# Suffix sums of stick-breaking attention: full fp32 products or split-operand products

## The chip, the cores and the metric

One core of a Trainium2 chip runs the whole kernel. The metric is device time in microseconds from launch to end; several runs are taken and the median is compared. The profile names the engines: PE (TensorE, matrix products) with its weight loads PEld, DVE (VectorE), ACT (ScalarE), POOL (GpSimd), SP (SyncE). Each engine works through its own list of instructions in order, and semaphores tie the lists together.

## What is computed

One layer of a streaming encoder for 512 new prompt frames and 32 frames of a running stream (with 512 cached keys and values). The input projection feeds gMLP gating and stick-breaking attention (8 heads of 64); an output projection and a mixture of 16 experts follow. The part that matters here:

```
def stick_breaking(q, k, v, q_pos, k_pos):
    z = jnp.einsum('bqhd,bshd->bhqs', q, k).astype(jnp.float32) * (SB_HEAD_DIM ** -0.5)
    causal = k_pos[None, :] < q_pos[:, None]
    log_beta = jax.nn.log_sigmoid(z)
    log_keep = jnp.where(causal, log_beta - z, 0.0)
    rest = lax.cumsum(log_keep, axis=3, reverse=True) - log_keep
    w = jnp.where(causal, jnp.exp(log_beta + rest), 0.0)
    return jnp.einsum('bhqs,bshd->bqhd', w.astype(v.dtype), v)
```

With s = softplus(z), the exponent of a weight is z minus the sum of s over this key and all later ones up to the query. So a reversed running sum over keys is needed for each query.

## The kernel before, in words

The kernel lies in one function, with one list of instructions per engine. Attention stands between the input projection (five column blocks, ends near 174 us in the profile) and the output projection (begins near 249 us).

Scores are kept transposed: keys on the 128 partitions, queries along the columns. There are nine passes, called heads here: pass 0 is the sample group with all its heads side by side, passes 1 to 8 are the eight prompt heads. For a prompt head the four key chunks of 128 need 512, 384, 256 and 128 query columns (causal), 1280 in all, in three PSUM banks: chunk 0 fills the first bank (512), chunks 1 and 3 the second (384 + 128), chunk 2 the third (256). Two sets of banks take turns, so the scores of head h+2 must wait until the weights of head h have been read out of the same banks.

For each head the steps are:

- scores (PE, L1475 and the mask product L1477): full fp32 products of the keys with the queries. A full fp32 product shows as two records of PE.
- absolute value (DVE, `abs_z`, L1000), then exp(-|z|) (ACT, L708) and log(1 + .) (ACT, L713) in `lw`; the 512-column bank first, then the other 768 columns.
- softplus (DVE, `softplus`, L1014): max(z, 0) plus that logarithm, from PSUM and SBUF into the tile `sp`; then three additions (L1030) that sum later key chunks for chunks that need more than one of them, into `later`.
- suffix sums (PE, `suffix_sums`): products of `negU` (-1 on and below the diagonal) with a chunk's own softplus (L1503, 1280 columns) and of `negones` (all -1) with the softplus of later chunks, summed by DVE where it can (L1513, 768 columns). They accumulate onto the scores in PSUM, all as full fp32 products.
- weights (ACT, `weights`, L782): exp of the banks into `lw`.
- values (PE, `values`, L1532, for pass 0 L1543): products of weights and values, for two heads at a time, half of them before each of the next heads' scores. ACT and DVE then write the result as a high and a low part (`sb_hi` L787, `sb_lo` L1089) for the output projection.

The order of PE in the loop over heads is written out by hand: part of the values of earlier heads (from head 4 on), scores of head h+1, suffix sums of head h; behind the loop the remaining values. DVE's order is absolute value and softplus of head h+1, and at heads 5 and 7 the low part of an attention output, at head 7 also a weight split. ACT's is exponentials and logarithms of head h+1, then weights of head h. POOL does nothing between 155 and 249 us. The weight loads of the experts on SP's queue start when the last values are done.

Projections already use split operands: an operand x is written as a high part of type fp32r (ACT, `whi`) and a low part x - high (DVE or POOL, `wlo`), and three products high x high, high x low, low x high replace one full fp32 product. Their products are L1384 to L1386; POOL's subtractions of low parts are L555 (512 columns), L564 (2048) and, in the expert stage, L591 (1024).

Of the kernel before, what the change touches and what calls it, by code (L numbers as in the profile page):

```python
# [34 lines left out]
def trunk_step(nc, x_prompt, x_sample, cache_k, cache_v, norm1_g, w_in, gm_v_norm_g, gm_w_s, gm_b_s,  # L35
# [34 lines left out]
    with ExitStack() as ctx:  # L70
# [19 lines left out]
        negU = sb("negU", [P, P])  # L90
        negones = sb("negones", [P, P])
# [37 lines left out]
        gvn = sb("gvn", [P, NT, CB], stack=mix)  # L129
# [13 lines left out]
        ZW = 1280  # L143
# [3 lines left out]
        sp = [sb(f"sp{i}", [P, ZW], stack=st_b) for i in range(2)]  # L147
        later = sb("later", [P, 6 * P], stack=st_b)
# [70 lines left out]
        later_ok = sem("later_ok")  # L219
# [60 lines left out]
        s_regions = [(c * DW // 512, c * DW % 512, DW, c) for c in range(NCH + 1)]  # L280
# [9 lines left out]
        def later_sums(h):  # L290
            return later[:, 3 * P * (h % 2):3 * P * (h % 2 + 1)] if h else later[:, :]
# [168 lines left out]
        def _(pool):  # L460
# [35 lines left out]
            link(pool.memset(negU[:, :], -1.0))  # L496
            pool.memset(negones[:, :], -1.0)
            pool.affine_select(out=negU[:, :], in_=negU[:, :], compare_op=ALU.is_ge, fill=0.0, base=0,
                               pattern=[[-1, P]], channel_multiplier=1).then_inc(pc, 1)
# [28 lines left out]
            for b in range(2):  # L528
# [3 lines left out]
                for t in range(NT):  # L532
# [6 lines left out]
                    pool.tensor_tensor(q3, q3, g, ALU.mult).then_inc(qk_ok, 1)  # L539

# [108 lines left out]
        def _(act):  # L649
# [52 lines left out]
            def exp_log(h):  # L702
                b_ = lw[h % 5]
                pieces = [[b_[:, 0:512]], [b_[:, 512:ZW]] if h else [b_[:, 512:1024], b_[0:DEC, 1024:ZW]]]
# [236 lines left out]
        def _(dve):  # L941
# [62 lines left out]
            def softplus(h):  # L1004
# [3 lines left out]
                s, u = sp[h % 2], later_sums(h)  # L1008
                if h == 0:
                    link(dve.memset(s[:, 1024:ZW], 0.0))  # L1010
# [6 lines left out]
                dve.wait_ge(sp_ok, h + 1)  # L1017


                n = P if h else DW  # L1020
                if h == 1:
                    dve.wait_ge(rest_ok, 2)
                if h:
                    adds = ((2, s[:, 1152:1280], s[:, 896:1024]), (1, s[:, 768:896], u[:, 2 * P:3 * P]),
                            (0, s[:, 640:768], s[:, 1024:1152]))
                else:
                    adds = ((2, s[:, 768:1024], s[:, 1024:1280]), (1, s[:, 512:768], u[:, 2 * n:3 * n]),
                            (0, s[:, 256:512], u[:, n:2 * n]))
                for k, a, b in adds:
                    ins = dve.tensor_tensor(u[:, k * n:(k + 1) * n], a, b, ALU.add)  # L1030
                    if k:
                        link(ins)
                ins.then_inc(later_ok, 1)
# [321 lines left out]
        def _(pe):  # L1355
# [102 lines left out]
            def scores(h):  # L1458
# [12 lines left out]
                if h:  # L1471
                    for bk, c0, n, c, q0 in regions:
                        if h >= 2 and c == 1:
# [5 lines left out]
                        if bk == 0:  # L1479
                            mm.then_inc(z_ok, 1)  # L1480
                else:
                    pe.wait_ge(ckT_ok, NCH)
                    for bk, c0, n, c in s_regions:
# [5 lines left out]
                        if c == 1:  # L1489
                            mm.then_inc(z_ok, 1)  # L1490
                    mm = pe.matmul(z[bk][0:DEC, c0:c0 + n], identb[0:DEC, 0:DEC], maskneg8[:, :, :].rearrange("p h n -> p (h n)"),
                                   start=False, stop=True, skip_group_check=True)
                mm.then_inc(z_ok, 1)

            def suffix_sums(h):

                z, s = z_of(h), sp[h % 2]
                pe.wait_ge(sp_ok, h + 1)
                pe.wait_ge(pc, PC_U)
                u = later_sums(h)  # L1500
                for bk, c0, n, c, *_ in (regions if h else s_regions):
                    p = P if h or c < NCH else DEC
                    pe.matmul(z[bk][0:p, c0:c0 + n], negU[0:p, 0:p], s[0:p, 512 * bk + c0:512 * bk + c0 + n],  # L1503
                              start=False, stop=True, skip_group_check=True)
                pe.wait_ge(later_ok, h + 1)
                if h:
                    rest = ((0, P, s[:, 512:512 + P]), (0, 2 * P, u[:, 0:2 * P]), (1, P, s[:, 1024:1024 + P]),
                            (1, 2 * P, u[:, 2 * P:3 * P]), (2, P, s[:, 896:1024]))
                else:
                    rest = ((0, 0, u[:, 0:DW]), (0, DW, u[:, DW:2 * DW]), (1, 0, u[:, 2 * DW:3 * DW]),  # L1510
# [241 lines left out]
```

## Time and profile before

| | us |
|---|---|
| median of 3 runs | 530.46 |
| lowest and highest run | 530.32, 533.29 |
| span of the profiled execution | 529.8 |
| PE, DVE, ACT, POOL busy in it | 448.5, 291.5, 241.3, 194.1 |
| mean granted clock of PE | 0.940 |

The page gives the profiled execution by its span, from the first to the last instruction; no separate time of that execution is shown, and the median of the runs is 0.66 us above the span. In a timeline row the first number is the start from the span's beginning, the second the time that the row covers, "xN" the number of instructions merged into it, and the bracket the idle time of that engine before it with what ended it. Consecutive matrix products overlap in their records, so their pace is read from start to start. "out<-in" are the program's tile names without buffer numbers; the tile `lw` appears as `ckT` and `cv` where these are reused for it.

### The profile page before, as it was taken

How to read it: one execution, taken by the hardware profiler on the slowest of the kernel's cores; microseconds unless marked ns; L12 is line 12 of the kernel's file. 1: busy time of each engine (PE TensorE's matmuls, PEld its weight loads, DVE VectorE, ACT ScalarE, POOL GpSimd, SP SyncE). 2: the span in 40 equal slices, each digit the busy share in tenths (PEclk: the TensorE clock that was granted, in tenths of full speed). 3: DMA queues.
4: the chain of work that ended last, by engine and by line, in shares of the span. 5: the costliest groups of instructions: out<-in, count | busy, mean ns of one | idle time of the engine just before them, and what ended most of it. 6: DMA issues, size and time to landing. Idle time of an engine off the chain costs nothing. (4 is left out here: it accounts for less than half of the span.)

```text
span 529.8 us, 7155 instructions
## 1 busy us (share of the span) xinstructions
PE 448.5 (85%) x2569; PEld 333.4 (63%) x2569; DVE 291.5 (55%) x411; ACT 241.3 (46%) x330; POOL 194.1 (37%) x189
## 2 busy tenths in 40 slices
PE   1899999998979899999999961689999999999300
PEld 1677887777758576656777861466766766666200
DVE  2626332443243446565150747269898898998136
ACT  4625121343333536456113531167787777876100
POOL 3442100474540000001000761266767767746261
PEclk9999999998979999999999986599999999999855
DMA  8547202222331300000297397359999999993267
GB/s 300 165 72 280 62 24 81 83 77 80 119 125 56 109 1 1 1 1 1 90 390 275 128 354 242 91 191 338 342 348 330 331 344 316 362 366 131 85 228 277
DMA packets 61700, 95.31 MB, mean 180 GB/s; under 512 B 9265, under 2 KB 42033, under 8 KB 61665
## 3 DMA queue, kind: packets, MB, share of 16 engines
q1 hardware_dynamic: 47040, 69.48, 38.7%
q0 software_dynamic: 5088, 17.89, 10.4%
q10 hardware_dynamic: 9536, 7.50, 4.3%
q8 instruction: 19, 0.31, 0.2%
q14 instruction: 17, 0.13, 0.1%
HBM read 81.82 MB, written 13.04 MB: 179 GB/s over the span
## 5 line engine op out<-in xcount | busy, mean ns | idle before, releaser
L1272 DVE TENSOR_TENSOR wlo<-raw,whi 128x2048 fp32r<-128x2048 f32 (+1 forms) x45 | 96.9, 2154 | 24.4 <-ACT whi L866 24.4
L1384 PE MATMUL bank<-whi,xT_hi 128*128 128x512 f32 x224 | 93.6, 418 | 2.5 <-issue 1.9
L1385 PE MATMUL bank<-wlo,xT_hi 128*128 128x512 f32 x224 | 90.8, 405 | 0.0
L1386 PE MATMUL bank<-whi,xT_lo 128*128 128x512 f32 x224 | 90.8, 405 | 0.0
L866 ACT ACTIVATE whi<-raw 128x2048 fp32r<-128x2048 f32 x45 | 86.0, 1912 | 6.2 <-PE bank L1386 6.2
L591 POOL TENSOR_TENSOR wlo<-raw,whi 128x1024 fp32r<-128x1024 f32 x16 | 59.6, 3724 | 34.4 <-ACT whi L866 34.4
L953 DVE TENSOR_TENSOR wlo<-raw,whi 128x2048 fp32r<-128x2048 f32 x14 | 32.0, 2287 | 52.6 <-ACT whi L657 52.6
L1384 PE MATMUL bank<-whi,xsT_hi 128*96 128x512 f32 x128 | 53.4, 417 | 4.4 <-DVE xsT_lo L1278 3.1
L1384 PEld LDWEIGHTS bank<-whi,xT_hi 128*128 128x128 f32 x224 | 43.6, 195 | 14.6 <-issue 4.2
L1386 PE MATMUL bank<-whi,xsT_lo 128*96 128x512 f32 x128 | 51.4, 402 | 0.0
L1385 PE MATMUL bank<-wlo,xsT_hi 128*96 128x512 f32 x128 | 51.3, 401 | 0.0
L1386 PEld LDWEIGHTS bank<-whi,xT_lo 128*128 128x128 f32 x224 | 43.7, 195 | 10.5
L1385 PEld LDWEIGHTS bank<-wlo,xT_hi 128*128 128x128 f32 x224 | 43.7, 195 | 9.2
L657 ACT ACTIVATE whi<-raw 128x2048 fp32r<-128x2048 f32 x14 | 26.7, 1908 | 45.5 <-PE bank L1406 43.1
L545 POOL MEMSET wr_pad<- 128x1024 f32 x1 | 1.0, 956 | 95.4 <-issue 95.4
L478 POOL TENSOR_SCALAR ssq<-ssq 128x1 f32<-128x1 f32 (+3 forms) x25 | 5.0, 201 | 79.7 <-DVE ssq L1063 47.7
L1384 PEld LDWEIGHTS bank<-whi,xsT_hi 128*96 128x96 f32 x128 | 21.0, 164 | 18.2 <-issue 7.1
L578 POOL COPY idx_cur<-idx_all 96x1 int32<-96x1 int32 (+1 forms) x16 | 20.1, 1255 | 21.3 <-PE bank L1644 11.4
L1384 PE MATMUL bank<-whi,aT_hi 128*96 128x512 f32 x64 | 26.1, 408 | 1.8 <-DVE aT_lo L1288 1.1
L1386 PEld LDWEIGHTS bank<-whi,xsT_lo 128*96 128x96 f32 x128 | 21.1, 165 | 9.3
L1385 PEld LDWEIGHTS bank<-wlo,xsT_hi 128*96 128x96 f32 x128 | 21.2, 166 | 7.1
L480 POOL TENSOR_TENSOR rstd<-ssq,mhalf 128x1 f32<-128x1 f32 (+3 forms) x25 | 24.7, 988 | 2.1
(214 smaller groups left out, 773.2 us busy)
## 6 DMA issues: line engine op xcount, KB each, us to landing
raw<-in_w_gate_dram SPq DMA_DIRECT2D x32, 512.0 KB, 6.3
raw<-in_w_up_dram SPq DMA_DIRECT2D x32, 512.0 KB, 7.8
raw<-in_w_down_dram SPq DMA_DIRECT2D x32, 512.0 KB, 7.2
raw<-in_w_in_dram SPq DMA_DIRECT2D x10, 1024.0 KB, 5.4
expert_rows<-yout POOLq DMA_DIRECT2D x16, 384.0 KB
raw<-in_w_out_dram SPq DMA_DIRECT2D x4, 1024.0 KB, 5.1
x_sb<-in_x_prompt_dram SPq DMA_DIRECT2D x4, 512.0 KB, 8.8
normed_tokens<-xn ACTq DMA_DIRECT2D x4, 512.0 KB, 2.7
```

What stands on the lines that cost most here:

```text
L478: link(pool.tensor_scalar(s, s, 1.0 / width, EPS, ALU.mult, ALU.add))
L480: return pool.tensor_tensor(dst, s, mhalf[0:s.shape[0], 0:n], ALU.pow)
L545: link(pool.memset(wr_pad[:, :, :], 0.0))
L578: pool.tensor_copy(idx_cur[p][:, :], idx_all[:, bass.ds(i, 1)]).then_inc(idx_cp, 1)
L591: pool.tensor_tensor(wlo[split][:, D:2 * D], eraw[slot][:, D:2 * D], whi[split][:, D:2 * D].bitcast(F32), ALU.subtract).then_inc(m_lo_pool, 1)
L657: act.activation(whi[n % 2][:, :], raw[n % 3][:, :], ACT.Copy).then_inc(hi_ok, 1)
L866: act.activation(whi[SPLIT_OF[m3]][:, :], eraw[slot][:, :], ACT.Copy).then_inc(m_hi, 1)
L953: dve.tensor_tensor(wlo[n % 2][:, :], raw[n % 3][:, :], whi[n % 2][:, :].bitcast(F32), ALU.subtract)\
L1272: dve.tensor_tensor(wlo[SPLIT_OF[m3]][:, 0:n], eraw[slot][:, 0:n], whi[SPLIT_OF[m3]][:, 0:n].bitcast(F32), ALU.subtract).then_inc(m_lo, 1)
L1384: pe.matmul(acc, x_hi, w_hi, start=start, stop=False)
L1385: pe.matmul(acc, x_hi, w_lo, start=False, stop=False)
L1386: return pe.matmul(acc, x_lo, w_hi, start=False, stop=stop)
```

## The change

The suffix sums become split-operand products; scores, values and everything else stay as they are.

- Softplus is written in place over the logarithm (`lw`). DVE copies it, rounded, to `s_hi` (fp32r). The low part `s_lo` is softplus minus `s_hi`: of the first bank ("head", 512 columns) by DVE, of the other two ("tail", 768 columns) by POOL. `negU` and `negones` become fp32r, their values being exact in it.
- The three additions on DVE are gone. Instead PE multiplies `negones` with the softplus of each later chunk separately, once with the high and once with the low part: 20 products per head instead of 9.
- The order is turned: tail first, head second, in scores, absolute values, exponentials, logarithms, softplus, sums and weights. Products are ordered so that those with the same stationary tile stand together.
- PE now waits for the high parts, for POOL's low part of the tail and for DVE's low part of the head. ACT's wait before the weights goes. The narrow own chunk of the sample group (32 keys) keeps a full fp32 product with a small triangle `negU_s`.
- `s_hi` and `s_lo` of odd heads lie where `gvn` was, so DVE waits before head 1's softplus for the transposes of `gvn` (`gm_tr`).

```
...
-        regions = [(0, 0, 512, 0, 0), (1, 0, 384, 1, 128), (1, 384, 128, 3, 384), (2, 0, 256, 2, 256)]
+        regions = [(1, 0, 384, 1, 128), (1, 384, 128, 3, 384), (2, 0, 256, 2, 256), (0, 0, 512, 0, 0)]
...
-            return [(0, P, slice(0, 512))] if a == 0 else [(1, P, slice(512, 1024)), (2, p, slice(1024, ZW))]
+            return [(0, P, slice(0, 512))] if a else [(1, P, slice(512, 1024)), (2, p, slice(1024, ZW))]
+        def stored_parts(h, a):
+            if a:
+                return [(P, slice(0, 512))]
+            return [(P, slice(512, ZW))] if h else [(P, slice(512, 1024)), (DEC, slice(1024, ZW))]
...
+            for h in range(NH):
+                pool.wait_ge(s_hi_ok, 2 * h + 1)
+                for p, c in stored_parts(h, 0):
+                    ins = pool.tensor_tensor(s_lo[h % 2][0:p, c], lw[h % 5][0:p, c], s_hi[h % 2][0:p, c].bitcast(F32), ALU.subtract)
+                ins.then_inc(s_lo_tail, 1)
...
             def weights(h):
-                act.wait_ge(sp_ok, h + 1)
...
                 if h >= 2:
                     dve.wait_ge(rest_ok, 2 * (h - 1))
+                elif h == 1:
+                    dve.wait_ge(gm_tr, NT)
+                b_, hi, lo = lw[h % 5], s_hi[h % 2], s_lo[h % 2]
                 for a in range(2):
                     dve.wait_ge(l_ok, 2 * h + a + 1)
                     for bk, p, c in parts_of(h, a):
-                        ins = dve.scalar_tensor_tensor(out=s[0:p, c], in0=z_of(h)[bk][0:p, 0:c.stop - c.start], scalar=0.0,
-                                                       in1=lw[h % 5][0:p, c], op0=ALU.max, op1=ALU.add)
-                ins.then_inc(sp_ok, 1)
...
-                for k, a, b in adds:
-                    ins = dve.tensor_tensor(u[:, k * n:(k + 1) * n], a, b, ALU.add)
...
+                        ins = dve.scalar_tensor_tensor(out=b_[0:p, c], in0=z_of(h)[bk][0:p, 0:c.stop - c.start], scalar=0.0,
+                                                       in1=b_[0:p, c], op0=ALU.max, op1=ALU.add)
+                    ins.then_inc(sp_ok, 1)
+                    dve.wait_ge(sp_ok, 2 * h + a + 1)
+                    for p, c in stored_parts(h, a):
+                        ins = dve.tensor_copy(hi[0:p, c], b_[0:p, c])
+                    ins.then_inc(s_hi_ok, 1)
+                dve.wait_ge(s_hi_ok, 2 * h + 2)
+                dve.tensor_tensor(lo[:, 0:512], b_[:, 0:512], hi[:, 0:512].bitcast(F32), ALU.subtract).then_inc(s_lo_head, 1)
...
             def suffix_sums(h):
+                def own(chunks, s):
+                    for c in chunks:
+                        bk, c0, n, q0 = place[c]
+                        mm = pe.matmul(z[bk][:, c0:c0 + n], negU[:, :], s[:, 512 * bk + c0:512 * bk + c0 + n],
+                                       start=False, stop=True, skip_group_check=True)
+                    return mm
+                def later(chunks, s):
+                    for c in chunks:
+                        bk, c0, n, q0 = place[c]
+                        for c2 in range(c + 1, len(place)):
+                            b2, d0, n2, q2 = place[c2]
+                            p = DEC if c2 == NCH else P
+                            at = c0 + q2 - q0
+                            mm = pe.matmul(z[bk][:, at:at + n2], negones[0:p, :], s[0:p, 512 * b2 + d0:512 * b2 + d0 + n2],
+                                           start=False, stop=True, skip_group_check=True)
+                    return mm
+                hi, lo = s_hi[h % 2], s_lo[h % 2]
+                tail, head = ((3, 2, 1), (0,)) if h else ((3, 2), (1, 0))
+                pe.wait_ge(s_hi_ok, 2 * h + 1)
+                own(tail, hi)
...
+                later(tail, hi)
+                pe.wait_ge(s_lo_tail, h + 1)
+                later(tail, lo)
+                own(tail, lo).then_inc(rest_ok, 1)
+                pe.wait_ge(s_hi_ok, 2 * h + 2)
+                own(head, hi)
+                later(head, hi)
+                pe.wait_ge(s_lo_head, h + 1)
+                later(head, lo)
+                own(head, lo).then_inc(rest_ok, 1)
...
```

## Rows read from the trace of the kernel before

**Rows 1.** Table of stretches: busy us (instructions) per engine, PEclk, DMA share, GB/s.

```profile
220.00:240.00 20.00, 20.00 (x102) 12.77 (x100) 11.15 (x23) 10.83 (x19) 0.00 (x0) 1.00 0.00 1
```

**Rows 2.** Timeline of one head: start, duration, engine, line; in brackets idle before.

```profile
219.33 1.12 PE L1475 MATMUL bank<-qpad,kT 128*128 128x512 f32 x2
...
220.62 0.69 DVE L1000 TENSOR_SCALAR lw<-bank 128x512 int32<-128x512 int32 x1 [0.76 <-PE bank L1477]
...
221.34 0.63 ACT L708 ACTIVATE lw<-lw 128x512 f32<-128x512 f32 x1 [2.26 <-DVE lw L1000]
...
221.98 2.38 PE L1503 MATMUL bank<-sp,negU 128*128 128x512 f32 x8
222.18 1.02 DVE L1000 TENSOR_SCALAR lw<-bank 128x512 int32<-128x512 int32 x2 [0.87 <-PE bank L1477]
...
223.24 0.84 ACT L708 ACTIVATE lw<-lw 128x768 f32<-128x768 f32 x1 [1.26 <-DVE lw L1000]
...
223.99 1.34 ACT L713 ACTIVATE lw<-lw 128x512 f32<-128x512 f32 x2
224.19 0.38 PE L1513 MATMUL bank<-sp,negones 128*128 128x128 f32 x2
...
224.70 1.69 DVE L1014 SCALAR_TENSOR_TENSOR sp<-bank,lw 128x512 f32<-128x512 f32 x3 [1.50 <-ACT lw L713]
...
225.61 0.64 PE L1532 MATMUL bank<-ckT,v_sb 128*64 128x512 f32 x1
...
226.84 0.70 PE L1475 MATMUL bank<-qpad,kT 128*128 128x512 f32 x1
```

**Rows 3.** Timeline of DVE: the absolute values of heads 3 and 8.

```profile
199.00 0.69 DVE L1000 TENSOR_SCALAR ckT<-bank 128x512 int32<-128x512 int32 x1 [0.18 <-PE bank L1477]
...
235.63 0.69 DVE L1000 TENSOR_SCALAR ckT<-bank 128x512 int32<-128x512 int32 x1 [0.76 <-PE bank L1477]
```

**Rows 4.** Timeline of PE: split-operand products of 512 columns, back to back.

```profile
172.06 0.40 PE L1384 MATMUL bank<-whi,xT_hi 128*128 128x512 f32 x1
172.30 0.40 PE L1385 MATMUL bank<-wlo,xT_hi 128*128 128x512 f32 x1
```

**Rows 5.** Groups of DVE by form, 160 to 260 us: the additions between SBUF tiles.

```profile
L1030 DVE TENSOR_TENSOR later<-sp 128x128 f32<-128x128 f32 x16 | 4.7, 292 | 0.5
...
L1030 DVE TENSOR_TENSOR later<-sp,later 128x256 f32<-128x256 f32 x2 | 0.8, 424 | 0.1
```

**Rows 6.** Groups of POOL by form: its low-part subtractions (busy us, mean ns).

```profile
L591 POOL TENSOR_TENSOR wlo<-raw,whi 128x1024 fp32r<-128x1024 f32 x16 | 59.6, 3724 | 34.4 <-ACT whi L866 34.4
...
L564 POOL TENSOR_TENSOR wlo<-raw,whi 128x2048 fp32r<-128x2048 f32 x2 | 9.0, 4508 | 4.1 <-ACT whi L809 4.1
...
L555 POOL TENSOR_TENSOR wlo<-raw,whi 128x512 fp32r<-128x512 f32 x4 | 5.1, 1278 | 0.0
```

**Rows 7.** Timelines of DVE and of POOL where both work on SBUF tiles.

```profile
295.97 2.30 DVE L1140 SCALAR_TENSOR_TENSOR xn<-x_sb,rstd,g2b 128x1024 f32<-128x1024 f32 x1 [0.40 <-POOL rstd L480]
298.94 0.69 DVE L1153 TENSOR_TENSOR x_sb<-x_sb,bank 128x512 f32<-128x512 f32 x1 [0.67 <-PE bank L1386]
...
303.73 1.26 DVE L1140 SCALAR_TENSOR_TENSOR xn<-x_sb,rstd,g2b 128x1024 f32<-128x1024 f32 x1
...
295.91 1.29 POOL L555 TENSOR_TENSOR wlo<-raw,whi 128x512 fp32r<-128x512 f32 x1
...
299.21 1.27 POOL L555 TENSOR_TENSOR wlo<-raw,whi 128x512 fp32r<-128x512 f32 x1
```

**Rows 8.** Timeline of PE: the values that follow the last head's sums.

```profile
245.53 1.72 PE L1532 MATMUL bank<-lw,v_sb 128*64 128x384 f32 x9
...
246.67 0.59 PE L1532 MATMUL bank<-ckT,v_sb 128*64 128x512 f32 x1
```

**Rows 9.** Timeline of PE at a long gap after attention; table of stretches behind it.

```profile
312.09 0.68 PE L1361 MATMUL bank<-ident,xn_late 32*128 32x32 f32 x8 [2.68 <-DVE xn_late L1140]
...
312.00:314.00 2.00, 1.91 (x14) 1.87 (x15) 0.12 (x2) 1.39 (x3) 0.00 (x0) 0.69 1.04 419
```

More of the change, by code:

```diff
@@ L142, in trunk_step @@
         st_b = ExitStack()
-        ZW = 1280
         lw = [sb(f"lw{i}", [P, ZW], stack=st_b)[:, :] for i in range(3)]
         lw += [x_[:, :, :].rearrange("p c n -> p (c n)")[:, 0:ZW] for x_ in (ckT, cv)]
-        sp = [sb(f"sp{i}", [P, ZW], stack=st_b) for i in range(2)]
-        later = sb("later", [P, 6 * P], stack=st_b)
+        s_hi = [sb("s_hi0", [P, ZW], F32R, stack=st_b)[:, :], s_hi1[:, :]]
+        s_lo = [sb("s_lo0", [P, ZW], F32R, stack=st_b)[:, :], s_lo1[:, :]]
         st_b.close()
@@ L275, in z_of @@
             return [bank[0], bank[1], bank[2]] if h % 2 else [bank[3], bank[4], bank[7]]
-        regions = [(0, 0, 512, 0, 0), (1, 0, 384, 1, 128), (1, 384, 128, 3, 384), (2, 0, 256, 2, 256)]
+        regions = [(1, 0, 384, 1, 128), (1, 384, 128, 3, 384), (2, 0, 256, 2, 256), (0, 0, 512, 0, 0)]
         DW = HEADS * DEC
-        s_regions = [(c * DW // 512, c * DW % 512, DW, c) for c in range(NCH + 1)]
+        s_regions = [(c * DW // 512, c * DW % 512, DW, c, 0) for c in (2, 3, 4, 0, 1)]
         NH = HEADS + 1
@@ L703, in exp_log @@
                 b_ = lw[h % 5]
-                pieces = [[b_[:, 0:512]], [b_[:, 512:ZW]] if h else [b_[:, 512:1024], b_[0:DEC, 1024:ZW]]]
+                pieces = [[b_[0:p, c] for p, c in stored_parts(h, a)] for a in range(2)]
                 for a in range(2):
@@ L1472, in scores @@
                     for bk, c0, n, c, q0 in regions:
-                        if h >= 2 and c == 1:
+                        if h >= 2 and bk == 0:
                             pe.wait_ge(w_ok, 2 * (h - 2) + 2)
@@ L1482, in scores @@
                     pe.wait_ge(ckT_ok, NCH)
-                    for bk, c0, n, c in s_regions:
+                    for bk, c0, n, c, _ in s_regions:
                         kt, p = (ckT[:, :, c * P:(c + 1) * P], P) if c < NCH else (kT[:, :, SEQ:TOK], DEC)
@@ L1505, in suffix_sums @@
[L1505 to L1510, printed above, removed]
-                            (1, DW, s[:, 1024:1024 + DW]))
-                for k, (bk, c0, a) in enumerate(rest):
-                    mm = pe.matmul(z[bk][:, c0:c0 + a.shape[-1]], negones[:, :], a, start=False, stop=True,
-                                   skip_group_check=True)
-                    if k == 1:
-                        mm.then_inc(rest_ok, 1)
@@ L1517, in suffix_sums @@
-                mm.then_inc(rest_ok, 1)
+                z = z_of(h)
+                place = {c: (bk, c0, n, q0) for bk, c0, n, c, q0 in (regions if h else s_regions)}
+                def own(chunks, s):
[4 more added lines that the diff above has]
+                    return mm
@@ new lines, in suffix_sums @@
+                hi, lo = s_hi[h % 2], s_lo[h % 2]
+                tail, head = ((3, 2, 1), (0,)) if h else ((3, 2), (1, 0))
+                pe.wait_ge(s_hi_ok, 2 * h + 1)
+                pe.wait_ge(pc, PC_U)
+                own(tail, hi)
+                if h == 0:
+                    bk, c0, n, _ = place[NCH]
+                    pe.matmul(z[bk][0:DEC, c0:c0 + n], negU_s[:, :], lw[0][0:DEC, 1024:ZW], start=False, stop=True,
+                              skip_group_check=True)
+                later(tail, hi)
@@ L1539, in values @@
                         hc = slice(j * P, (j + 1) * P)
[L1540 removed]
+                        for bk, c0, n, c, _ in sorted(s_regions, key=lambda x: x[3]):
                             vv, p = (cv[:, c, hc], P) if c < NCH else (v_sb[0:DEC, NT - 1, hc], DEC)
```

59 lines of the change are left out of this document (21 added, 38 removed).

## The prediction

> **What bounds the kernel now.** I read three views in this order. The table of stretches, for where the changed sums stand (181 to 249 us): between 220 and 240 PE is busy all 20 us, DVE and ACT some 11 each, POOL not at all, at full clock [rows 1]. Then the timeline of one head there, for who waits for whom [rows 2]. PE goes without a gap from scores (219.33) to the sums of the head before (221.98), to values (225.61) and the next scores (226.84): 7.51 us. DVE works in pieces: absolute value of the first 512 columns, a wait for PE, that of the other 768, a wait of 1.50 for ACT, softplus, three additions. Last, DVE's starts alone: from the absolute value of head 3 to that of head 8, five heads take 235.63 - 199.00 = 36.63 us [rows 3]. So PE sets the pace, and DVE's waits are the reserve that the change can spend. The reader should see that DVE's order is a closed loop: it takes up head h+1 only when the last operation of head h's softplus is done, and within a head it must wait for ACT. Of its 7.51 us only the two waits for PE, 0.76 and 0.87, are free.
>
> **What the change saves on PE.** Now 1280 columns with the triangle take 224.19 - 221.98 = 2.21 us and 768 with the ones 225.61 - 224.19 = 1.42 [rows 2]: 3.63 per head. Afterwards a head has 20 split-operand products: 8 of 128 columns, 6 of 256, 4 of 384, 2 of 512, in all 5120 columns. Such products of 512 columns start 0.24 apart now [rows 4], which would be 2.4 us in proportion. None of 128 columns is in the trace. From below it costs its share, 0.06; from above what 128 columns of a full product cost, 1.42 / 6 = 0.24. I take half of that, 0.12, since each full product is two halves with a weight load each. Sum: 8 x 0.12 + 6 x 0.12 + 4 x 0.18 + 2 x 0.24 = 2.9 us, 0.7 less per head; by the ends 2.4 and 3.8. Head 0 has 28 such products of 256 columns and saves about as much. Over nine heads PE would gain some 6.5 us if it stayed the bound.
>
> **What it adds on DVE and POOL.** The three additions go (0.29 each [rows 5], 0.96 with gaps). In their place DVE writes the high part twice (768 and 512 columns) and subtracts for the low part of 512; POOL subtracts for the 768. The price of the copy is not in the trace. From above, an SBUF operation at one column per cycle: 0.292 for 128 columns and 0.424 for 256 [rows 5], so 0.13 per 128: 0.95 for 768 and 0.69 for 512. From below, the fixed part alone, 0.16. I take the upper end, the nearest row, and 0.69 for DVE's subtraction too. POOL: 1.278 for 512 columns, 4.508 for 2048 [rows 6], 2.10 ns a column, so 1.82 for 768.
>
> What decides is that POOL and DVE do not run freely side by side. A DVE operation of 1024 columns with two SBUF inputs takes 1.26 when POOL is idle (303.73), but 2.30 when it starts 0.06 after a POOL subtraction of 1.29: it waits for that one's end, 297.20, and then takes 1.07 [rows 7]. One with a PSUM input is not held: 0.69 at 298.94, although POOL's next subtraction begins at 299.21 [rows 7]. So DVE's softplus of the second half (PSUM and SBUF) and, at one column per cycle, its second copy go on beside POOL, but its subtraction (two SBUF inputs) stands until POOL is done.
>
> DVE's loop, from rows 2 and these prices: absolute value of 768 columns 1.02; ACT until the first logarithm 0.04 + 0.84 + 0.63 + 0.84 - 2 x 0.09 (a logarithm put at the exponential's price; ACT's operations overlap, 223.24 + 0.84 against 223.99) + 0.10 = 2.27; softplus of 768 1.02; copy 0.98 with its gap; hand-over to POOL 0.08 (an estimate between the 0.03 and 0.10 from engine to engine in rows 2); POOL 1.82, under which DVE's 0.69 + 0.69 are hidden; subtraction 0.72. Sum 7.91, say 7.9. With the copy at its lower end it is 7.1. The wait for ACT is longer than now because the larger half goes first: two exponentials and one logarithm of 768 columns stand in it. PE's work per head is 1.23 (values) + 2.65 (scores) + 2.9, 6.8; ACT's own loop, from scores to the weights that free the banks of the scores after them, is some 6.5 by the same rows. **The bound moves from PE (7.51) to DVE with POOL (7.9).**
>
> One rule of the Trainium skill bears on the copy. VectorE: DVE Perf Modes, section "The perf-mode tier table", gives an fp32 copy within SBUF two columns per cycle, in a mode that takes both of DVE's read ports. No row here shows such a copy. By that page's figures the copies would be an estimated 0.46 and 0.33, the loop 7.4 to 7.8 (7.8 if the second copy has to stand behind POOL as well), and the total 1 to 3 us less than mine.
>
> **The sum along the path.** Head 0's sums get shorter, but the weights that free the next scores now come after a larger first half: scores of head 2 start some 0.4 later. The sums of head 1 give back 0.7. The absolute value of head 3 then waits for 768 columns of scores instead of 512, 0.6 more. It starts at 199.00 + 0.4 - 0.7 + 0.6 = 199.3. Then five loops of 7.9, and once the low part of an attention output on DVE (0.7), which now has no wait to hide in: head 8 at 239.5 instead of 235.63. POOL's part of head 8 ends 7.18 later (7.9 less the subtraction): 246.7. Behind it on PE stand the tail's low products, the head's high and the head's low ones, 0.7 each and ready by then: 248.8, where the sums end at 245.53 now [rows 8]. A part of the values follows (1.1), then the last values at 249.9 instead of 246.67: **+3.2 us**. Everything after (projections, experts, their loads) waits for these and moves with it. What stands behind the added waits: on PE, behind the wait for POOL's part, the head's products, counted above; on POOL nothing, its next work comes after attention; ACT loses one wait. POOL's one more constant (0.3) comes long before its use. The tiles of odd heads lie where the gated rows were; the wait for this is for transposes that end before head 1's softplus. Profiled span 529.8 + 3.2 = 533.0; the runs' median lies 0.66 above that span, so 533.7.
>
> **Rivals.** (a) POOL and DVE do not hold each other here. Then DVE's loop is 7.44 with my copies and 6.1 with the lowest, where PE (6.8) is the bound. With the lowest, five loops of 6.8 and the 0.7 bring head 8 to 234.0, POOL's part ends 6.4 later, 240.4, the three groups of products at 242.5, and the last values start at 243.6: 3.1 us less than now, 527.4. With my copies it comes to 531.4. For it: POOL is idle in the whole stage. Against it: rows 7 show the hold. (b) The 128-column product costs 0.24. Then head 1's sums save nothing (+0.9) and the three groups at the end are 0.9 longer: +5.0, 535.5. The other loops are still DVE's (PE 1.23 + 2.65 + 3.8 = 7.7). (c) POOL takes its long form. In the expert stage 1024 columns take 3.72 [rows 6], 2.79 for 768, where the slope would give 1.82. It decides if a DVE operation with two SBUF inputs gets in ahead of POOL's; 0.08 after the copy DVE is in one with a PSUM input, which speaks against. Price 0.97 in each of five loops and at the end: +9.0, 539.5. (d) PE's clock: an idle gap of some 1.1 us in each loop is new. One of 2.68 stood before a stretch of two us at a mean of 0.69 [rows 9]; ours is less than half of that. A fall would cost at most some 2 us a time.
>
> **Chances.** My case, with any copy, 0.66; (a) 0.16; (b) 0.10; (c) or (d) 0.08. A measurement of this kernel can tell about 1%, 5.3 us, from no change. Faster by more (under 525.2) needs more than the quick end of (a): 0.05. Slower by more (over 535.8) takes (c), (d), half of (b) or a longer loop in my own case: 0.18. Within 1%: 0.77. My own case reaches from 529 (lowest copies: 0.8 less in each loop and at the end, 4.7 in all) to 535. The range goes from a little below (a)'s quick end to between (b) and (c): 526.5 to 537.5.
>
> **What would show it.** Right: DVE's period at 7.4 to 7.9 between heads 3 and 8; POOL busy 1.8 per head; DVE's low subtraction of 512 columns, or the copy before it, long, because it starts while POOL runs and ends after it; PE with gaps of about a microsecond before scores; 2.4 to 2.9 us of PE for a head's sums. Wrong: PE gapless with a period under 7; a low subtraction of 0.69 in the middle of POOL's; 128-column products 0.2 apart.

## The result: slower by 10 us, beyond the range

The changed kernel takes 541.3 us (538.8 to 543.1, four runs), the kernel before 531.2 beside it: ratio 1.017 [1.0136, 1.0204]. The forecast was 533.7, its range ended at 537.5. The profiled execution has a span of 539.5 us against 529.8, and a granted clock of 0.921 against 0.940. Cut at two marks on PE, the last short transposes of `gvn` ahead of head 0's sums and the first product of the output projection, the 9.7 us between the spans are:

| stretch | before | after | difference |
|---|---|---|---|
| start to the last transposes of `gvn` | 180.76 | 178.39 | -2.4 |
| from there to the output projection | 68.15 | 77.57 | +9.4 |
| from there to the end | 280.9 | 283.5 | +2.6 |

The forecast had 0, +3.2 and 0 there. The first stretch of the page to look at is the sums of head 0. In the table of stretches after the change (columns as in [rows 1]) the clock is the last number but two:

```profile
177.00:181.00 4.00, 3.09 (x17) 1.84 (x16) 3.09 (x6) 2.04 (x4) 0.00 (x0) 1.00 0.02 7
181.00:185.00 4.00, 4.00 (x14) 2.84 (x13) 2.65 (x5) 2.44 (x5) 1.02 (x1) 0.53 0.00 0
185.00:189.00 4.00, 4.00 (x12) 2.80 (x12) 1.77 (x2) 0.51 (x1) 0.79 (x1) 0.50 0.00 0
189.00:192.00 3.00, 3.00 (x11) 1.84 (x10) 0.41 (x1) 0.09 (x1) 0.00 (x0) 0.59 0.00 0
192.00:196.00 4.00, 4.00 (x31) 3.59 (x28) 2.39 (x6) 3.36 (x7) 0.00 (x0) 1.00 0.01 4
...
220.00:240.00 20.00, 16.98 (x101) 11.18 (x100) 14.84 (x24) 11.47 (x22) 4.36 (x3) 1.00 0.00 0
```

PE is fully busy from 181 to 192 us, but at 0.50: the lower of its two levels, 1.2 GHz. In steps of 1 us the fall begins at 181.2 and lasts 10.2 us; a second one of 3.4 us stands at 249.5. The kernel before has neither. The last line answers [rows 1]: PE, busy all 20 us then, now idles 3.

PE's timeline after the change, where the clock falls:

```profile
178.39 0.40 PE L1366 MATMUL bank<-ident,gvn 32*128 32x32 f32 x4 [0.91 <-DVE xT_lo L1111]
178.72 0.50 PE L1510 MATMUL bank<-s_hi,negU 128*128 128x256 f32 x2
179.16 0.61 PE L1533 MATMUL bank<-lw,negU_s 32*32 32x256 f32 x2
179.70 1.01 PE L1522 MATMUL bank<-s_hi,negones 32*128 32x256 f32 x3
180.55 0.97 PE L1522 MATMUL bank<-s_lo,negones 32*128 32x256 f32 x3
181.45 0.80 PE L1510 MATMUL bank<-s_lo,negU 128*128 128x256 f32 x2
...
182.47 2.58 PE L1522 MATMUL bank<-s_hi,negones 128*128 128x256 f32 x7
...
188.26 1.48 PE L1480 MATMUL bank<-qpad,kT 128*128 128x384 f32 x2
...
192.35 0.47 PE L1510 MATMUL bank<-s_hi,negU 128*128 128x128 f32 x2
```

Ahead of the fall stand a gap of 0.91, transposes of 32x32, and products whose operands have only 32 rows: the sample group's fifth key chunk has 32 keys. The same place in the kernel before:

```profile
180.76 0.40 PE L1361 MATMUL bank<-ident,gvn 32*128 32x32 f32 x4 [0.91 <-DVE xT_lo L1106]
181.09 2.54 PE L1503 MATMUL bank<-sp,negU 128*128 128x256 f32 x10
...
185.68 1.13 PE L1475 MATMUL bank<-qpad,kT 128*128 128x512 f32 x2
...
188.33 2.38 PE L1503 MATMUL bank<-sp,negU 128*128 128x512 f32 x8
```

The sums take 188.26 - 178.72 = 9.54 us, 4.59 before, and the scores of head 2 4.09, 2.65 before.

The loop over the prompt heads, which the forecast was about, answers to [rows 2, 3, 7]:

```profile
217.78 0.65 PE L1510 MATMUL bank<-s_hi,negU 128*128 128x128 f32 x3
...
218.36 1.61 DVE L1016 TENSOR_SCALAR lw<-bank 128x512 int32<-128x512 int32 x3
...
219.41 1.37 ACT L725 ACTIVATE lw<-lw 128x768 f32<-128x768 f32 x2 [3.82 <-DVE lw L1016]
...
220.73 1.30 PE L1559 MATMUL bank<-lw,v_sb 128*64 128x384 f32 x8
...
221.61 1.02 DVE L1030 SCALAR_TENSOR_TENSOR lw<-bank,lw 128x512 f32<-128x512 f32 x2 [1.64 <-ACT lw L730]
...
222.66 0.56 DVE L1035 CAST s_hi<-lw 128x768 fp32r<-128x768 f32 x1
...
222.83 0.91 PE L1480 MATMUL bank<-qpad,kT 128*128 128x384 f32 x2 [0.81 <-ACT cv L798]
...
223.14 0.68 DVE L1030 SCALAR_TENSOR_TENSOR lw<-bank,lw 128x512 f32<-128x512 f32 x1
...
223.30 1.81 POOL L555 TENSOR_TENSOR s_lo<-lw,s_hi 128x768 fp32r<-128x768 f32 x1 [5.87 <-DVE s_hi L1035]
...
223.86 1.54 DVE L1035 CAST s_hi<-lw 128x512 fp32r<-128x512 f32 x1
...
225.44 0.69 DVE L1038 TENSOR_TENSOR s_lo<-lw,s_hi 128x512 fp32r<-128x512 f32 x1
...
226.05 1.61 DVE L1016 TENSOR_SCALAR lw<-bank 128x512 int32<-128x512 int32 x3
```

DVE is the bound, as forecast: 226.05 - 218.36 = 7.69 us a head, PE waits some 0.8 in each, and a head's sums take it 220.73 - 217.78 = 2.95 (forecast 2.9). The 768-column copy takes 0.56, the 512-column one 1.54: it begins 0.56 after POOL's subtraction (223.30) and ends 0.29 after that one's end (225.11).

### The profile page after: what moved, and what is told of

Same layout as the page of the kernel before. It is cut to its first block and busy times, and to the rows that moved or that the text cites. A ratio compares the mean times of both kernels' runs of the same rounds, so it can differ in the third digit from the quotient of the medians.

```text
span 539.5 us, 7212 instructions
## 1 busy us (share of the span) xinstructions
PE 449.8 (83%) x2597; PEld 339.0 (63%) x2597; DVE 305.9 (57%) x411; ACT 240.4 (45%) x330; POOL 208.9 (39%) x200
## 5 line engine op out<-in xcount | busy, mean ns | idle before, releaser
L1390 PE MATMUL bank<-wlo,xT_hi 128*128 128x512 f32 x224 | 89.7, 401 | 0.0
L1391 PE MATMUL bank<-whi,xT_lo 128*128 128x512 f32 x224 | 89.5, 400 | 0.0
L555 POOL TENSOR_TENSOR s_lo<-lw,s_hi 128x768 fp32r<-128x768 f32 (+2 forms) x7 | 11.2, 1610 | 59.5 <-DVE s_hi L1035 59.5
L1480 PE MATMUL bank<-qpad,kT 128*128 128x384 f32 (+3 forms) x64 | 23.5, 491 | 4.6 <-ACT lw L798 2.9
```

The lines of the kernel that those rows point to most:

```text
L555: ins = pool.tensor_tensor(s_lo[h % 2][0:p, c], lw[h % 5][0:p, c], s_hi[h % 2][0:p, c].bitcast(F32), ALU.subtract)
L1390: pe.matmul(acc, x_hi, w_lo, start=False, stop=False)
L1391: return pe.matmul(acc, x_lo, w_hi, start=False, stop=stop)
L1480: pe.matmul(z[bk][:, c0:c0 + n], kT[:, (h - 1) // 2, c * P:(c + 1) * P], qpad[:, h - 1, q0:SEQ], start=(c0 == 0), stop=True, skip_group_ch ...
```

## The experiments

A head is called a pass in the expectations; pass 0 is the sample group. "gvn to out" is the stretch of the second line above in the run's own profile, 68.15 in the kernel before, which has no fall there. The ratio is to the kernel before on the same chip (its medians 530.95 to 532.43), with its 95% interval.

| kernel | us | ratio, 95% | half clock in pass 0: from, us | gvn to out |
|---|---|---|---|---|
| after_again | 540.5 | 1.0166 [1.0128, 1.0205] | 181.7, 10.2 | 77.57 |
| pool_late | 538.95 | 1.0134 [1.0105, 1.0162] | 181.5, 10.2 | 77.76 |
| late_head | 537.6 | 1.0134 [1.0067, 1.0201] | 181.5, 10.2 | 76.12 |
| fill | 536.7 | 1.0070 [1.0032, 1.0109] | 180.5, 10.2 | 76.81 |
| pad | 532.3 | 1.0028 [1.0002, 1.0053] | none | 71.38 |
| pad2 | 534.5 (one) | | none | 71.31 |
| pad_tail | 533.3 | 1.0049 [1.0005, 1.0092] | none | 73.56 |
| head0_full | 544.1 | 1.0244 [1.0190, 1.0297] | 179.1, 10.2 | 79.54 |
| late2_fill | 530.5 | 0.9986 [0.9951, 1.0021] | 179.1, 10.2 | 71.28 |
| late2_pad | 527.5 | 0.9948 [0.9919, 0.9978] | 179.9, 3.4 | 65.80 |
| late2_fill_pad | 526.0 | 0.9901 [0.9864, 0.9938] | none | 65.04 |
| best_again | 524.5 | 0.9887 [0.9840, 0.9934] | none | 65.03 |
| before_fill | 529.8 | 0.9979 [0.9950, 1.0007] | none | 68.15 |
| before_shift | 530.6 | 0.9979 [0.9951, 1.0007] | 177.1, 10.2 | 72.52 |
| before_shift2 | 535.4 (one) | | 179.1, 10.2 | 72.49 |
| before_shift_fill | 529.3 | 0.9955 [0.9933, 0.9977] | none | 68.16 |
| after_unshift | 541.6 | 1.0155 [1.0107, 1.0203] | 183.2, 13.7 | 78.15 |

**Is the fall chance?** The changed kernel, nothing edited.

> The changed kernel once more, nothing edited. The profile of it shows PE at half clock from about 181 to 191.5 us, over head 0's sums (9.5 us instead of some 4) and the scores behind them. If that belongs to the changed kernel: again near 541, and again a half-speed stretch there. If it was the chance of one execution: some runs near 534 with a mean clock above 0.935, and no such stretch in this profile.

Measured 540.5; the fall stands at 181.7 us and takes 10.2 again. It belongs to the kernel.

**The hold between POOL and DVE.** Two ways out. POOL waits until DVE's low part is through (pool_late):

```
                 pool.wait_ge(s_hi_ok, 2 * h + 1)
+                pool.wait_ge(s_lo_head, h + 1)
```

> POOL's subtraction waits until DVE has written the low part of the head, so that the two never meet. If POOL holds DVE's copy: the 512-column copy takes 0.4 instead of 1.54, DVE's period between heads 3 and 8 falls from 7.68 to 6.6 to 6.9 (PE's own 6.75 is then the bound), and the time by 4 to 5 us, to 536 or 537. Rival, the copy is slow by itself: 1.5 us as before, period 7.7, 541.

Or DVE's second copy and its low part move behind the next head's absolute values (late_head):

```
+                    if a:
+                        continue
                     for p, c in stored_parts(h, a):
                         ins = dve.tensor_copy(hi[0:p, c], b_[0:p, c])
...
                     abs_z(h + 1)
+                if h:
+                    head_parts(h)
+                if h + 1 < NH:
                     softplus(h + 1)
```

> DVE makes the head's high and low part of head h only behind the absolute value of head h+1, in its wait for ACT. If DVE's closed loop with POOL's hold is the bound: period from 7.68 to about 6.8 (PE), the copy at 0.4 or less, 4 to 5 us less, 536 to 537. Rival, the loop is not the bound (ACT's chain or PE at 7.5 is): period 7.5 or more and within 1 us of the unedited time.

With POOL later, DVE's second copy takes 0.43 instead of 1.54: the hold is real, and the copy is what waits. Five heads take 34.96 us, 39.01 after the change. (Absolute values, which read PSUM, begin inside POOL's subtraction there, at 217.33 with POOL busy from 216.63 to 218.44, and take 1.62, as they do without it: this kind is not held, as [rows 7] were read.) With the copies moved five heads take 33.66, 6.7 each, and PE waits only once, 0.73: it is the bound. But little of that reached the end, 538.95 and 537.6 where 536 to 537 were expected. POOL's part of the last head came later, and PE's second half-clock stretch, at 246 us, grew from 3.4 to 6.8 us; in late_head the last head's parts also stood behind a weight split on DVE, an oversight of mine, mended in the later versions (late2: for the last head `head_parts` directly follows its softplus). Both kept the fall in head 0.

**Are the gaps to blame?** The scores of head 1 go in portions between the transposes of `gvn`, into the gaps of 1.07 and 0.91 us:

```
-            scores(1)
+            scores(1, (0,))
             for t in range(NT):
+                if t == 2:
+                    scores(1, (1, 2))
+                if t == 4:
+                    scores(1, (3,))
```

> The scores of head 1 are put in three portions between the transposes of the gated rows, where PE waits 1.07 and 0.91 us just ahead of head 0's sums; nothing else changes. If these gaps bring the clock down: no half-speed stretch there, head 0's sums about 4.2 us instead of 9.5 and the scores of head 2 at 2.65 instead of 4.1, and the gaps' 2 us saved: 541 to about 532. Rival, the narrow or split products themselves let the clock fall: the stretch stays and only the gaps' 2 us go, 539.

0.29 us of the gaps is left in its profile, and the fall is there all the same. So this fall needs next to no idle time; two of the six runs, 533.9 and 532.5 at mean clocks of 0.937 and 0.943, may have gone without it.

**Are the 32-row products?** In pad, chunk 4 of head 0 is filled up with zeros, as in the kernel before, and no product with `negones` has 32 rows any more; in head0_full its products stay narrow, but are full fp32.

```
                 if h == 0:
+                    for x_ in (s_hi[0], s_lo[0]):
+                        link(dve.memset(x_[:, 1024:ZW].bitcast(F32), 0.0))
...
-                            p = DEC if c2 == NCH else P
+                            p = P
```

> Chunk 4 of pass 0 (32 rows of keys) is padded to 128 rows of zeros in the high and the low parts, so the eight products of pass 0 with a 32-row operand become 128-row products, as before the change; nothing else moves. Theory N (the narrow products bring the clock down): sums of pass 0 at the full clock, 4.5 to 5.5 us in place of 9.54, scores 2 at 2.7, the time some 6 us under the changed kernel's 540.5, 533 to 535.5. Theory S (a row of split products, 29 of them one behind the other without a gap, brings it down, however many rows they have): the stretch at the half clock of about 10 us from 181 us on stays, 539.5 to 541.5. Two memsets more on VectorE cost under 0.3 us by either.

```
+                if h == 0:
+                    hi, negU_of, ones_of = lw[0], negU[:, :].bitcast(F32), negones[:, :].bitcast(F32)
...
+                if h == 0:
+                    own(tail[-1:], hi)
+                else:
+                    later(tail, lo)
+                    own(tail, lo).then_inc(rest_ok, 1)
```

> Pass 0 alone takes its sums as full fp32 products of the softplus itself (5 own and 10 later ones of 256 columns, the 32-row operands kept; its high and low parts are still made, unused but for the waits). Passes 1 to 8 keep the split products. The nine full products of pass 0 before took 4.59 us, 0.51 each, so 15 take 7.6 us at the full clock, 2 less than the 9.54 that the split ones took at half of it. Theory S (split products): no half clock in pass 0, sums 7.6 to 8.2, scores 2 at 2.7, the time 537 to 538.5; the fall may come in a later pass instead, then 540 or more. Theory N (narrow operands): the half clock stays from about 181 us on, the sums take 12 or more, the time 543 or more.

The padding takes the fall away in both of its profiles, and 7 to 8 us of the time (0.0138 of the ratio). None of its eleven executions took more than 535.1 us, none of the changed kernel's eight less than 538.8. The padded products also run faster, so whether the clock falls for the few rows or for the slow pace, these runs do not tell apart. PE's timeline of the padded kernel, to be set beside the one above:

```profile
176.85 0.41 PE L1369 MATMUL bank<-ident,gvn 32*128 32x32 f32 x4 [0.91 <-DVE xT_lo L1114]
177.18 0.51 PE L1513 MATMUL bank<-s_hi,negU 128*128 128x256 f32 x2
...
178.16 0.62 PE L1525 MATMUL bank<-s_hi,negones 128*128 128x256 f32 x3
178.62 0.52 PE L1525 MATMUL bank<-s_lo,negones 128*128 128x256 f32 x3
178.98 0.40 PE L1513 MATMUL bank<-s_lo,negU 128*128 128x256 f32 x2
...
179.45 1.00 PE L1525 MATMUL bank<-s_hi,negones 128*128 128x256 f32 x7
...
181.96 0.91 PE L1483 MATMUL bank<-qpad,kT 128*128 128x384 f32 x2 [0.43 <-ACT lw L798]
```

The sums take 4.78 us with the wait, the scores after them 2.62. head0_full gave the 544 of its theory N, but not by its mechanism: there the clock fell at 179.1, in the last gap, ahead of any sum. It does not tell the two theories apart.

**Four of the eight.** In pad_tail only the four narrow products right behind the transposes are padded (`p = DEC if c2 == NCH and c < 2 else P`).

> Only four of the eight products with 32 rows are padded, those right behind the short transposes of gm, where the clock fell; the other four stay, among 14 wide ones. If narrow products bring the clock down only where they stand close to idle time and to each other: as the full padding, 532 to 534. If any four do it: the fall comes some 3 us later, and the time is 538 to 541.

No fall in pass 0 in its one profile: the other four, among wide ones, did not bring it about there. Two of its seven runs, 536.1 and 537.6 at mean clocks of 0.934 and 0.931, may have met one. The four are slow even at the full clock:

```profile
178.61 0.40 PE L1513 MATMUL bank<-s_lo,negU 128*128 128x256 f32 x2
...
179.08 1.56 PE L1525 MATMUL bank<-s_hi,negones 128*128 128x256 f32 x7
180.58 1.67 PE L1525 MATMUL bank<-s_lo,negones 128*128 128x256 f32 x7
...
182.52 0.81 PE L1483 MATMUL bank<-qpad,kT 128*128 128x384 f32 x2
```

The row "x7" holds two products with 32 rows and takes 1.50 to the next group (180.58), the padded seven 0.84 (179.45 to 180.29). (Its 73.56 holds a fall of 6.8 us in the last head's sums, at 241; in pad and pad2 one of 3.4 stands there.)

**Gaps and narrow products with the loop mended.** late2_fill has the copies moved and the gaps filled, the narrow products left; before_fill is the kernel before with the gaps filled.

> VectorE's copy and low part of the head columns come behind the next pass's absolute values, so that VectorE's turn with the port no longer lies under GpSimd's low part; for the last pass they follow its softplus directly; and the scores of pass 1 stand between the transposes of gm, in the two gaps there. The loop runs at TensorE's pace, 6.8 us a pass (33.7 us for five passes in the run with the late head, 39.0 in the changed kernel). Theory S: pass 0 stays at the half clock for about 10 us, the end of attention 2 us earlier than in the run with the late head and 2 from the filled gaps: 537.6 - 4 = 533.6, within 532 to 535. If the gaps and the loop's rhythm made the fall: no half clock in attention, 526 to 528.

> The kernel before, with the scores of pass 1 between the transposes of gm: a control for what the two filled gaps are worth alone. They are 2 us of idle TensorE there, as after; theory: 1.5 to 2.5 us off, 529 to 530, at an unchanged clock (0.940). Rival: with the gaps gone pass 0 meets the fall of the clock too, and the gain goes: 531 to 535.

late2_fill took 530.5, under the 532 to 535 expected with a fall. It has almost no idle time there: 0.41 us in the 20 ahead of 180 us, and the fall begins at 179.1, among the narrow products, which start at 177.56. Over the next 20 us PE is busy throughout, at a clock of 0.77:

```profile
160.00:180.00 20.00, 19.59 (x129) 14.57 (x128) 10.31 (x18) 10.61 (x22) 2.16 (x2) 0.98 0.32 109
180.00:200.00 20.00, 20.00 (x96) 15.01 (x95) 7.85 (x17) 5.76 (x12) 3.62 (x2) 0.77 0.00 1
```

```profile
177.56 1.00 PE L1538 MATMUL bank<-s_hi,negones 32*128 32x256 f32 x3
178.40 0.95 PE L1538 MATMUL bank<-s_lo,negones 32*128 32x256 f32 x3
```

before_fill took 1.5 us less, about what was expected, but its interval includes no change.

**All three repairs, and two of them.**

> All three repairs: VectorE's head copies behind the next absolute values, the scores of pass 1 in the gaps, chunk 4 of pass 0 padded to 128 rows. Without the padding this version took 530.5 with about 10 us at the half clock in pass 0; the padding alone took 8 us off the changed kernel. Theory (idle TensorE and narrow operands together bring the clock down, each of them is now gone): no half clock between 170 and 300 us, five passes in 34 us, 523 to 526, under both kernels and under the kernel before with its gaps filled (529.8). Rival (the split products bring it down once they come without a pause): a stretch at the half clock somewhere in attention, 528 or more.

> As the last one, without the scores in the gaps: what the loop at TensorE's pace is worth at the full clock. The padded kernel took 532.3 with 7.7 us a pass in the loop; at 6.8 five passes save 4.5 to 5, and the end of attention keeps it: 527 to 528. If the saving is given back at the end, as when GpSimd came late, 530 or more. The gaps of 0.9 to 1.1 us ahead of pass 0 stay, so the clock may still fall in some executions.

526.0 and 527.5, both under the kernel before by 0.5 to 1%, with intervals that leave out 1. Without the fill (late2_pad) a fall of 3.4 us is left in pass 0. It covers a row of seven padded products, which take 1.50 us at half the clock:

```profile
180.08 1.70 PE L1537 MATMUL bank<-s_hi,negones 128*128 128x256 f32 x7
181.58 1.70 PE L1537 MATMUL bank<-s_lo,negones 128*128 128x256 f32 x7
```

**The 2.4 us ahead of attention.** The input projection is the same code in both kernels, yet it ran faster. The groups of PE by form from 34 to 116 us (last number ahead of the idle time: mean ns of one), of the kernel before, after the change, and of the kernel before with 128 unused bytes a partition where the change puts `negU_s`:

```profile
L1385 PE MATMUL bank<-wlo,xT_hi 128*128 128x512 f32 x95 | 37.5, 394 | 0.0
```

```profile
L1390 PE MATMUL bank<-wlo,xT_hi 128*128 128x512 f32 x96 | 37.4, 390 | 0.0
```

```profile
L1386 PE MATMUL bank<-wlo,xT_hi 128*128 128x512 f32 x96 | 37.4, 390 | 0.0
```

From start to start the products stand 0.2333 us apart before and 0.2267 after (35 and 37 products between 36 and 44 us).

```
         negones = sb("negones", [P, P])
+        sb("spare", [DEC, DEC])
```

> The kernel before with a spare tile of 32x32 fp32 (128 bytes a partition) between the constant matrices, where the change has its negU_s; nothing uses it, and all tiles behind it, xT_hi and xT_lo among them, lie 128 bytes further on, as after the change. In the untouched projections the 512-column products stand 0.2333 us apart in both kernels of the before family and 0.2267 in every one of the after family, and the short transposes of q end 2.2 us earlier. Theory (the place of the tiles sets the pace): 0.2267 here too, the short transposes of q at 118.7 to 119.7 in place of 120.9, the time 528 to 529.5. Rival (the pace comes from something else in the changed program, such as its length or its code's place): 0.2333 and 530.5 to 531.5.

0.2267, and the short transposes of q at 118.4 (120.9 before): the place of the tiles sets the pace. But the time fell by 0.9 only, within the noise, where 528 to 529.5 was expected, for this kernel, without a split product in its sums, met the fall too. In its two profiles attention takes 72.52 and 72.49 us, 4.4 more than without a fall; by its time not all ten runs, at mean clocks of 0.934 to 0.945, are likely to have met it. In its second profile:

```profile
179.45 0.60 PE L1362 MATMUL bank<-ident,gvn 32*128 32x32 f32 x4 [0.91 <-DVE xT_lo L1107]
179.98 4.77 PE L1504 MATMUL bank<-sp,negU 128*128 128x256 f32 x10
184.68 2.93 PE L1514 MATMUL bank<-later,negones 128*128 128x256 f32 x6
```

Here the full products with the triangle take 4.70 us to the next group, nearly twice their 2.46 at the full clock (177.48 to 179.94 in before_shift_fill). So I had to ask again whether the change was caught by its own products, or because it begins attention earlier. after_unshift puts `negU_s` behind `ckT` and `cv`, by which `xT_hi` and `xT_lo` lie as before; before_shift2 and pad2 repeat two kernels for a second profile.

> The changed kernel with the 128 bytes of negU_s put behind ckT and cv, so that xT_hi and xT_lo lie where they lay before the change; no instruction changes. The projections should run at the pace of before, 0.2333 us a product, and attention begin some 2.2 us later, by which its quiet moments meet the chip's look at TensorE at another point. Theory N2 (idle time and narrow products bring the clock down alike; the changed kernel has so much of both ahead of and in pass 0 that it is caught wherever the look falls): the half clock comes in the sums of pass 0 here too, the time 541 to 544. Rival P (only where the look falls matters, and the change moved it there by 128 bytes): no half clock in pass 0, 535 to 538.

> The kernel before with the spare 128 bytes once more, for a second profile: in the first one the clock fell at 177.3 us, inside the last gap of gm's transposes, and the sums of pass 0 ran at half of it for 10.2 us. If the place of the gaps decides, it falls here too, at the same point within 0.5 us; if it is chance from one execution to the next, it may not.

> The padded kernel once more, for a second profile: in the first one attention ran at the full clock throughout. By theory N2 no half clock between 165 and 200 us, about 532; if the first profile was a lucky execution, a stretch of about 10 us there and 537 or more.

All three came as expected: the unshifted kernel falls, for 13.7 us (its products are back at 0.2323 us), the shifted kernel before falls again in its last gap, the padded one does not. So the changed kernel was not caught because attention begins earlier. Narrow products with next to no idle time (late2_fill) can bring the fall, and so can the gaps without a narrow product with `negones` (before_shift, twice). Neither does so each time: the kernel before, pad and pad2 have the same gaps of 1.07 and 0.91 us and no fall in pass 0. What decides there, no run shows.

**What the split is worth by itself.** before_shift_fill has the spare bytes and the filled gaps, best_again is late2_fill_pad once more.

> The kernel before with both things that it can have without the split: the spare 128 bytes (projections at 0.2267 a product, 2.2 us) and the scores of pass 1 in the gaps of gm's transposes (2 us of idle time, and with it the fall of the clock that the shift alone met). Theory N2: no half clock in pass 0, from gm's short transposes to the output projection 68.2 us as in the kernel before, the time 4 under it: 526.5 to 528. Rival: the clock falls in pass 0 all the same (then full fp32 sums meet it without any gap), 531 or more.

> The version with all three repairs again, next to the last one on the same chip: with the layout and the gaps equal, what is left between the two is the split itself. From gm's short transposes to the output projection it took 65.04 us where the kernel before takes 68.15, so 3.1 less: 523.5 to 526 here, 2 to 3.5 under the other. If the rest of the kernel eats it, within 1 us of the other.

No fall in pass 0 in either profile. With the layout and the gaps equal the split kernel is 4.8 us faster, 524.5 against 529.3 by ratios of 0.9887 and 0.9955 to the kernel before; 2 to 3.5 were expected, and before_shift_fill missed its 526.5 to 528. In attention the profiles differ by 3.1 (68.16 - 65.03), and that much is shown to be the split's. Another 1.3 stands behind attention (281.6 and 280.3), in a part that varies without an order; and seven of before_shift_fill's ten runs, at mean clocks of 0.932 to 0.934 against 0.938 in its profile, may have met a fall that the profile does not have. One head of best_again shows why:

```profile
207.27 1.81 POOL L555 TENSOR_TENSOR s_lo<-cv,s_hi 128x768 fp32r<-128x768 f32 x1 [4.65 <-DVE s_hi L1040]
...
209.11 1.62 DVE L1016 TENSOR_SCALAR lw<-bank 128x512 int32<-128x512 int32 x3 [1.32 <-PE bank L1500]
...
210.65 0.42 DVE L1045 CAST s_hi<-cv 128x512 fp32r<-128x512 f32 x1
...
211.10 0.69 DVE L1047 TENSOR_TENSOR s_lo<-cv,s_hi 128x512 fp32r<-128x512 f32 x1
```

While POOL subtracts (207.27 to 209.08), DVE finishes a softplus that reads PSUM and waits for PE; its copy of 512 columns comes later and takes 0.42.

## Why the prediction was wrong

**The step that failed is the clock, rival (d), and beside it the price of head 0's products.** The prediction priced a fall at "at most some 2 us a time", expected it at the loop's new gaps and gave it, with (c), 0.08. The loop's gaps of 0.8 us brought none: the clock is 1.00 in the lines from 192 to 196 and 220 to 240 us. It came in head 0, which the prediction passed over in one sentence, "Head 0 has 28 such products of 256 columns and saves about as much", without asking how many rows these have. Eight have 32. Between the same marks the changed kernel takes 77.57 and the padded one 71.31 and 71.38: 6.2 us. The narrow products' own pace is 1.9 of it: 0.9 ahead of the fall (178.72 to 181.45 against 177.18 to 178.98 in pad) and 0.9 in the rest of the sums, as pad_tail shows them at the full clock (178.61 to 182.52 against 178.98 to 181.96 in pad). The clock is the other 4.4: 2.9 in the rest of the sums (181.45 to 188.26 against pad_tail's 3.91) and 1.5 in the scores of head 2 (4.09 against 2.62). So the fall cost over twice its price, and the pace of the narrow products stood in the sum with nothing. That [rows 9] showed a mean of 0.69 over two us was read as the price of a whole fall; it was the edge of one, which lasts 3.4 us from 312.8 on.

**The rest of the sum came out right, in part by luck.** Without the fall in head 0, in the padded kernel, attention takes 3.16 to 3.23 us more than before; the forecast was 3.2. Its milestones in pad2, moved by the 2.11 us by which its last transposes come earlier: absolute value of head 3 at 199.1 (forecast 199.3), of head 8 at 238.1 (239.5), last values at 249.8 (249.9). That the last agrees is luck: the loop was 0.2 a head shorter than forecast, and the last head's sums met a fall of 3.4 us that was not in the sum, so that 11.7 us follow on head 8 for the 10.4 forecast.

**The loop.** 7.69 for 7.91. The first copy with its hand-over took 0.64 (222.66 to 223.30), not 1.06: the upper end of the price was the wrong one. The second copy, which I had running on beside POOL, was held, and the subtraction begins 0.33 after POOL's end (225.11) instead of at once. The rule that I set beside my price, of the Trainium skill (VectorE: DVE Perf Modes, "The perf-mode tier table"), gave 0.46 and 0.33 and a loop of 7.8 with the second copy held; the trace has 0.56, 0.42 when free, and 7.69. It agrees in the pace, 0.14 for 256 columns, and in the loop; each copy took 0.1 more than the estimate. What the hold looks like is in the Trainium skill (SBUF — State Buffer, "SBUF: two separate sides"): DVE in a mode with two ports, or with two SBUF inputs, and GpSimd take the shared pair in turn and whole. The runs agree: 1.54 beside POOL, 0.43 when POOL waits.

**What the sum left out.** Tiles that move: the projections ran 2.4 us faster, a gain that the change did not mean to make. And the 2.6 us behind attention, which I cannot place: the changed kernel has 30.7 us at half clock there, the kernel before 23.9, and this may be part of it, but pad has 23.9 too and takes 1.0 longer there than the kernel before. Over all the kernels of this study that part takes 279.4 to 283.5 us in no order that follows from an edit. It stays open, as does why the kernel before, with the same gaps as its shifted form, shows no fall in pass 0 in its one profile. Nine of the 83 runs of it beside the experiments have a mean clock of 0.938 or less and take 532.8 to 535.8 us; they may have met one. A smaller error: the forecast added 0.66 us to the span, but a run's time lies 1.8 to 2.0 above its own span (541.42 and 539.5).

## What to carry to other kernels

Price PE's clock where the work is thinnest, not only where the new gaps are: behind products with few rows the clock fell here although PE shows as busy, and ran 10 us at half speed. Fill such operands up with zeros and put other work into short gaps ahead of them; a split that looked 10 us slower was then faster than its like, by 3.1 us in attention and 4.8 by the medians. And measure a change against a kernel with the same layout, since 128 bytes a partition moved the projections by 2 us.

## What had not been expected of the hardware

- The clock fell with PE busy 19.59 of the 20 us ahead (late2_fill, fall from 179.1), and padding the narrow operands took the fall away. The Trainium skill (TensorE: Matmul & The Clock Gate, "Part 1: The HAM clock gate") ties the clock to how busy the engine has lately been; the busy share of the profile alone did not foretell the fall here.
- A row in which products of 32 and of 128 rows alternate is slow in itself. At the full clock two with 32 rows and a wide one between them take 180.55 - 179.70 = 0.85 us, the same three padded 178.62 - 178.16 = 0.46. Whether the few rows cost this or the change between the two kinds, no run tells.
- 128 bytes of SBUF a partition ahead of `xT_hi` change the pace of a 512-column split product from 0.2333 to 0.2267 us, on unchanged code.
- The two costs come nearly as a product: seven products of 256 columns, padded, take 0.84 us at the full clock and 1.50 at half of it (late2_pad); with two of them narrow, 1.50 at the full clock (pad_tail) and 2.51 at half (182.47 to 184.98 after the change). Each alone is 1.8 times, both together 3.0.
